# A hybrid streaming layer on one core: the opening with one 96-column product and chunked fill, and the router tile by tile in the output projection

## What is computed

```
h  = RMSNorm(x);  p = h @ W_in            # columns for all branches: qi (1024), ki (64), wi (16), g_lr (16), ...
o_A = sparse attention: scores sum_h wi[t,h] relu(qi[t,h] . ki[s]), top-k keys, softmax over them
o_G = gated linear attention, forget gate from g_lr (rank 16);  o_M = attention into 256 memory tokens
x1 = x + W_out( sum_b sigmoid(gate_b(h)) * (o_b @ W_b) )
y  = x1 + HMoE(RMSNorm(x1))   # top-1 of 4 expert groups, then top-2 of its 8 experts; 32 experts of 3 MB
...
g_logit = hb @ w_group_router + b_group_router;  g_idx = argmax(g_logit)
e_logit = (hb @ w_expert_router + b_expert_router)[group g_idx];  top_p, top_i = top_k(softmax(e_logit), 2)
```

## Time and profile before

| | |
|---|---|
| median of 3 runs | 1762.69 us |
| profiled execution, own time | 1760.87 us |
| its span | 1759.2 us |
| PE busy | 1545.2 us (88%) |
| DVE, ACT, POOL busy | 529.0, 296.1, 109.5 us |
| mean DMA rate | 144 GB/s |

### The profile page before, as it was taken

How to read it: one execution, slowest core, us unless ns; L and a number is a source line. 1 busy time by engine, 2 the same in 40 slices (tenths; PEclk the granted TensorE clock), 3 DMA queues, 4 the chain that set the end, 5 groups by cost and what they waited for, 6 DMA issues and landing times.

```text
span 1759.2 us, 16947 instructions
## 1 busy us (share of the span) xinstructions
PE 1545.2 (88%) x6653; PEld 862.2 (49%) x6653; DVE 529.0 (30%) x1462; ACT 296.1 (17%) x689; POOL 109.5 (6%) x176
## 2 busy tenths in 40 slices
PE   3999999999799999988999999999999728878771
PEld 3554555445455544465555445755544524444440
DVE  3204489205400032442010343244640330101013
ACT  4004310212200011143100112343000201110100
POOL 5000000012000000000000100100000020000002
PEclk9899999999899999999999999999999758998996
DMA  9971121111332325134114130220150347999995
GB/s 259 214 209 37 37 54 31 48 48 49 108 96 72 119 96 191 48 130 158 49 50 141 49 125 11 74 82 27 48 190 5 143 172 278 422 422 421 422 421 201
DMA packets 131256, 253.13 MB, mean 144 GB/s; under 512 B 9840, under 2 KB 87664, under 8 KB 116848
## 3 DMA queue, kind: packets, MB, share of 16 engines
q1 hardware_dynamic: 114352, 183.03, 29.2%
q0 software_dynamic: 16832, 69.12, 12.2%
HBM read 214.21 MB, written 37.91 MB: 143 GB/s over the span
## 4 chain that ended last, share of the span: by engine, by line
PE 76%; DMA 12%; DVE 5%; ACT 3%; issue 2%; POOL 1%; SPq 1%; DVEq 0%; ACTq 0%; POOLq 0%
PE ps L656 21%; DMA arena<-slot_rows 9%; PE ps L678 7%; PE ps L577 6%; PE ps L587 6%; PE ps L606 3%; PE ps L626 3%; PE ps L565 3%; PE ps L1151 2%; PE ps L578 2%; PE ps L588 2%; PE ps L679 2%; PE ps L701 1%; PE ps L1130 1%; PE ps L1054 1%
## 5 line engine op out<-in xcount | busy, mean ns | idle before, releaser
L656 PE MATMUL ps<-bulk 128*128 128x512 f32 x848 | 373.5, 598 | 4.4 <-issue 4.4
L656 PEld LDWEIGHTS ps<-bulk 128*128 128x128 f32 x848 | 160.2, 192 | 196.9 <-issue 196.9
L577 PE MATMUL ps<-bulk 128*128 128x512 f32 x256 | 133.7, 604 | 3.8 <-DMA bulk<-in_w_in 3.8
L678 PE MATMUL ps<-bulk 128*128 128x512 f32 x256 | 135.1, 609 | 0.0
L587 PE MATMUL ps<-arena,bulk 128*128 128x512 f32 x256 | 131.1, 594 | 1.8 <-DVE arena L1660 1.8
L1130 PE MATMUL ps<-bulk,arena 128*64 128x256 f32 x1024 | 116.4, 386 | 9.1 <-DMA bulk<-in_w_exp_gate 8.3
L1130 PEld LDWEIGHTS ps<-bulk,arena 128*64 128x64 f32 x1024 | 81.6, 139 | 49.4 <-issue 22.1
L1151 PE MATMUL ps<-bulk,arena 128*64 128x512 f32 x256 | 71.5, 709 | 11.2 <-ACT arena L1515 11.2
L578 PEld LDWEIGHTS ps<-bulk 128*128 128x128 f32 x256 | 49.4, 193 | 62.6 <-issue 62.6
L1117 PE MATMUL ps<-cst,arena 128*128 128x128 f32 x128 | 20.2, 309 | 66.6 <-DMA arena<-slot_rows 66.6
L679 PEld LDWEIGHTS ps<-bulk 128*128 128x128 f32 x256 | 48.6, 190 | 61.2 <-issue 61.2
(11 more groups left out here) (364 smaller groups left out, 1932.8 us busy)
## 6 DMA issues: line engine op xcount, KB each, us to landing
bulk<-in_w_exp_gate SPq DMA_DIRECT2D x32, 1024.0 KB, 22.5
bulk<-in_w_exp_up SPq DMA_DIRECT2D x32, 1024.0 KB, 24.6
bulk<-in_w_exp_down SPq DMA_DIRECT2D x32, 1024.0 KB, 23.1
bulk<-in_w_in SPq DMA_DIRECT2D x48, 512.0 KB, 5.1
bulk<-in_w_in SPq DMA_DIRECT2D x7, 2048.0 KB, 10.6
slot_rows<-arena POOLq DMA_DIRECT2D x1, 13056.0 KB, 68.1
bulk<-in_w_mem_kv SPq DMA_DIRECT2D x4, 2048.0 KB, 9.5
arena<-slot_rows SPq DMA_DIRECT2D x16, 512.0 KB, 25.9
```

The source lines that it names most:

```text
L577: mm(ps[4 * q + 1][:, 0:TP], tw[2 * q][:, k, :], hT[:, k, 0:TP], start=k == 0, stop=k == KD - 1)
L656: last = mm(ps[4 + n % 2][:, :], lhs[:, k, tok:tok + P], ring[f % 2][:, k, :], start=k == 0, stop=k == KD - 1)
L678: mm(ps[b][:, 0:TP], tw[s][:, k, :], hT[:, k, 0:TP], start=k == 0, stop=k == KD - 1)
```

## The change

**Opening.** On SP the gain `g_x` is issued right behind tile 0, the narrow weights come as three DMAs (`g_lr`, `wi`, `ki`, in this order side by side), and the memory tiles are issued behind the first four indexer blocks. Each token tile has a semaphore of its own, so ACT squares each when it lands. DVE scales tiles 0 and 1, then 2 to 4. PE transposes these five, then makes one product with the 96 narrow columns as the stationary operand (result 96 x tokens), indexer block 0, five small transposes that bring the result back to tokens x 96, block 1, the transposes of the memory tiles, blocks 2 and 3, the transposes of `kid`, and blocks 4 to 7. ACT squares all `ki` at once, and DVE makes one `rstd` and a few wide operations for all five tiles.

**Fill.** The zeros for `slot_rows` go out in 17 DMAs, number c behind narrow block c of the score stage (the last two behind block 15).

**Router.** In the second half of the output projection DVE scales tile t as soon as ACT has squared it; PE puts the transposes of tile t - 1 behind item t and the logits of tile t - 2 into the middle of item t. After the last item the logits of tile 3, the transposes and the logits of tile 4 remain. DVE chooses experts for tiles 0 to 3 and then for tile 4 (`route`), and the rank products of the first four tiles are made between the two. For tile 4 and the totals a sum over four tiles (`hot_sum`) replaces four products by one. `pos_ok` is raised once when the row numbers stand and again after the overflow tables; the softmax weights w0 and w1 are made last. POOL's tables (`iota`) are made after the left half of the projection instead of after all of it.

The diff, cut to what the text speaks of:

```diff
+            for at, col, w in ((0, C_LR, RANK), (RANK, C_WI, HI), (RANK + HI, C_KI, DI)):
+                sp.dma_start(wsm[:, :, at:at + w], w_in[:, :, col:col + w]).then_inc(wsm_in, 16)
...
+            for t in range(NT):
+                x_transposes(t)
+            pe.wait_ge(hT_ok, 2 * NT)
+            pe.wait_ge(wsm_in, 48)
+            for k in range(KD):
+                mm(ps[4][0:NF3, 0:TP], wsm[:, k, :], hT[:, k, 0:TP], start=k == 0, stop=k == KD - 1)
+                last = mm(ps[5][0:NF3, 0:TS], wsm[:, k, :], hT[:, k, TP:T], start=k == 0, stop=k == KD - 1)
+            last.then_inc(kiw_full, 1)
+            indexer_block(0)
...
-            for t in range(NT):
-                if t >= 2:
-                    pe.wait_ge(kid_ok, t - 1)
-                for k in range(KD):
-                    last = mm(ps[2 + t % 2][:, 0:DI + HI], hT[:, k, t * P:(t + 1) * P], wsm[:, k, 0:DI + HI],
-                              start=k == 0, stop=k == KD - 1)
-                last.then_inc(kiw_full, 1)
...
+            for n in index["out"]:
...
+                for k in range(KD):
+                    if c and k == KD // 2 and t >= 2:
+                        if t == 2:
+                            pe.wait_ge(rtw_in, 5 * 16)
+                        router_logits(t - 2)
...
+                if c and t:
+                    h2_transposes(t - 1)
+            router_logits(NT - 2)
+            h2_transposes(NT - 1)
+            router_logits(NT - 1)
...
+            dve.wait_ge(rtw_in, 80)
             for n in index["out"]:
...
+                if c:
+                    ffn_normed(t)
+
+            dve.wait_ge(rt_full, 1)
+            dve.wait_ge(pool_step, 2 + N_TABLES)
+            route(0, NT - 1)
+            dve.wait_ge(rt_full, 2)
+            route(NT - 1, NT)
...
-            g.dma_start(slot_rows.rearrange("(p n) d -> p n d", p=CAP), zrow[0:CAP, :].unsqueeze(1).to_broadcast([CAP, N_SLOT, D]))\
-             .then_inc(fill_ok, 16)
...
+            for c in range(FILLS):
+                j = min(c, 2 * KD - 1)
+                pool.wait_ge(t_full[j % 4], U_QK + j // 4 + 1)
```

More of the change, by code:

```diff
@@ L394, in _ @@
             for t in range(NT):
[L395 to L399, removed]
+                sp.dma_start(xt[:, t, :], x_tile[t]).then_inc(X_IN[t], 16)
+                if t == 0:
+                    sp.dma_start(g_x, a["attn_norm_g"].partition_broadcast(P)).then_inc(gx_in, 16)
+            for at, col, w in ((0, C_LR, RANK), (RANK, C_WI, HI), (RANK + HI, C_KI, DI)):
+                sp.dma_start(wsm[:, :, at:at + w], w_in[:, :, col:col + w]).then_inc(wsm_in, 16)
             def narrow_job(col, u):
@@ L544, in _ @@
[L544 to L567, removed]
+            def indexer_block(j):
+                s, u, b = j % 4, U_QI + j // 4, 2 * (j % 2)
+                pe.wait_ge(tw_in[s], 16 * u)
+                pe.wait_ge(t_free[(s + 2) % 4], u + 1 if s >= 2 else u)
+                for k in range(KD):
+                    mm(ps[b][:, 0:TP], tw[s][:, k, :], hT[:, k, 0:TP], start=k == 0, stop=k == KD - 1)
+                    last = mm(ps[b + 1][:, 0:TS], tw[s][:, k, :], hT[:, k, TP:T], start=k == 0, stop=k == KD - 1)
+                last.then_inc(t_full[s], 1)
@@ new lines, in _ @@
+            for t in range(NT):
+                last = tr(ps[6][:, t * NF3:(t + 1) * NF3], featT[:, t * P:(t + 1) * P], ident[0:NF3, 0:NF3])
+            last.then_inc(kiw_full, 1)
+            indexer_block(1)
+            pe.wait_ge(glr_ok, 1)
+            for m in range(NM):
+                x_transposes(NT + m)
+            indexer_block(2)
+            indexer_block(3)
+            pe.wait_ge(kid_ok, 1)
+            pe.wait_ge(hT_ok, 2 * (NT + NM))
+            for t in range(NT):
+                last = tr(ps[(7, 4)[t // 4]][:, (t % 4) * P:(t % 4 + 1) * P], kid[:, t, :], ident)
@@ L569, in merge_job @@
+            last.then_inc(kidT_full, 1)
+            for j in range(4, KD):
+                indexer_block(j)
+            pe.wait_ge(const_ok, N_CONST)
             def merge_job(u, m, ready, before_branch=None):
@@ L1080, in _, with h2_transposes @@
             pe.wait_ge(merged_ok, 16)
-            project(("out",))
-            n = 0
-            for t in range(NT):
+            def h2_transposes(t):
                 pe.wait_ge(h2_ok, t + 1)
                 for h in range(2):
+                    n = 2 * t + h
                     if n >= 2:
@@ L1100, in _ @@
-            pe.wait_ge(rt_step, 2)
-            for t in range(NT):
-                for s in range(t + 1):
-                    mm(ps[3][:, t * NE:(t + 1) * NE], before if s == t else ones, hot_both[:, s, :], start=s == 0, stop=s == t)
-            for s in range(NT):
-                last = mm(ps[3][:, NT * NE:(NT + 1) * NE], ones, hot_both[:, s, :], start=s == 0, stop=s == NT - 1)
-            last.then_inc(rank_full, 1)
+                    last = mm(lt_bank(t), h2T[:, k, t * P:(t + 1) * P], w_rt[:, k, :], start=k == 0, stop=k == KD - 1)
@@ new lines, in _ @@
+            router_logits(NT - 2)
+            h2_transposes(NT - 1)
+            router_logits(NT - 1)
+            rank = ps[6]
+            pe.wait_ge(rt_step, 1)
+            for t in range(NT - 1):
+                for s in range(t + 1):
+                    mm(rank[:, t * NE:(t + 1) * NE], before if s == t else ones, hot_both[:, s, :], start=s == 0, stop=s == t)
+            pe.wait_ge(rt_step, 2)
+            t = NT - 1
+            mm(rank[:, t * NE:NT * NE], ones, hot_sum, start=True, stop=False)
@@ L1107, in _ @@
+            mm(rank[:, t * NE:NT * NE], before, hot_both[:, t, :], start=False, stop=True)
+            mm(rank[:, NT * NE:(NT + 1) * NE], ones, hot_sum, start=True, stop=False)
+            mm(rank[:, NT * NE:(NT + 1) * NE], ones, hot_both[:, t, :], start=False, stop=True).then_inc(rank_full, 1)
             pe.wait_ge(pos_ok, 1)
@@ L1200, in _, with x_squared @@
                 act.sem_inc(t_free[s], 1)
-            for t in range(NT + NM):
-                act.wait_ge(x_in[min(t, 2)], 16 if t < 2 else 16 * (NT + NM - 2))
+            def x_squared(t):
+                act.wait_ge(X_IN[t], 16 if t < NT else 16 * NM)
                 if t:
@@ L1581, in _ @@
+            dve.wait_ge(kid_ok, 1)
             dve.wait_ge(hT_ok, 2 * (NT + NM))
```

277 lines of the change are left out of this document (168 added, 109 removed).

## The result

| | before | after |
|---|---|---|
| median of the runs, us | 1760.4 (1756.7 to 1765.1) | 1712.2 (1707.7 to 1713.4) |
| ratio, 95% interval | | 0.972 (0.969 to 0.975) |
| profiled execution, span | 1759.2 | 1706.0 |
| scores start | 132.8 | 109.1 |
| projection starts | 1301.2 | 1273.4 |

The change takes 48 us off the median and brings it to 1712.2, where 1711 was forecast. Before was run once more beside after, which is why its median is 1760.4 here and not 1762.7. Two single executions are left out of the medians that follow, because they ran far from the others of their kernel and no trace shows why: 1777.9 us of before with the new router stage, and 4110.7 us of the combined kernel.

A forecast was written before the change was run, and what follows sets the result against it. PE is busy 88% of the span, except in a DMA-full opening and a serial stage before the scatter. 1759.2 - 25.5 (opening) - 26.0 (router) = 1707.7 span, 1711 us median; range 1703 to 1720 (0.74), to 1730 (0.86).

The forecast's parts named there:

- Tile 4 lands at 14.0: Opening: the sample tile lands at 14.0 us, since g_x ahead of it leaves the bytes ahead about the same.
- To the product at 24.1: Opening: square, rstd, three scalings, eight transposes and a copy after tile 4 lands let the 96-column product start at 24.1.
- Eight blocks and the inserted work, 73.6: Opening: eight indexer blocks 69.2 us, plus 4.4 for inserted transposes and a memory-tile wait; scores at 107.4.
- Narrow weights landed in time: Opening: narrow weights land at about 18 to 21 us, needed at 24.1, cover 3 us.
- Fill at 0: 13 MB zero fill beside the narrow blocks at 133 to 313 us: cost 0, at most 5 in the last rounds.
- The middle moves as a block: Between 133 and 1301 us nothing is tied to an absolute time; order unchanged, so it moves as a block.
- Last item 78.9 after the projection's start: Projection: inserted transposes and logits add 8.3 us, so the last item ends at 1380.1 instead of 1371.8.
- Give-back behind the scatter, 1.0: Behind the scatter: expert 3's 3 MB issued 2.1 us later against it; 1.0 of the 27.0 gain given back.
- Late opening: Rival, opening: tile 4 at 19 and product at half clock give 5 + 7.6 us back, 1724; chance 0.12.
- Clock inside the projection: Rival, projection: 36-column products halve the clock for three items, 28 us back, 1739; chance 0.07.
- Weights eat the gain: Rival, experts: weights' bytes limit from 1372 us on, so an earlier scatter buys nothing, 1737; chance 0.03.
- slower by the fill: Rival, narrow blocks: fill gets ahead of their weights; all 68.1 us on PE's path gives 1779; chance 0.02.

The follow-up runs named there:

- the combined kernel: After, with g_x in POOL's queue, narrow weights in two transfers, extra identity transposes in the opening and 216 behind the last rank: 1711.8 us, ratio 0.972.

## Why the prediction was right, point by point

- **Tile 4 lands at 14.0: wrong, 15.9.** The step that failed is "the bytes ahead are about the same". They are, but g_x had moved from a queue beside the tiles into the queue of the tiles; moved back, the tile lands at 13.2 with the same bytes.
- **To the product at 24.1: 27.4.** Of the 3.3 us, 1.9 is the landing; the rest is the transposes of three tiles, 5.7 us at half clock behind one another, where I counted only the last at 1.9.
- **The product, 9.7: 8.7.** Full clock from its first record. The 96 stationary columns cost no more than 128 (8.65 a block).
- **Eight blocks and the inserted work, 73.6: 73.0.** So the scores came at 109.1 instead of 107.4 and the opening gave 23.7 instead of 25.5 us.
- **Narrow weights landed in time: right.** They landed 12.0 and 7.6 us after their issue, and PE never waited. The Trainium skill (DMA: Bandwidth & Descriptors, Specifications) asks for at least 512 B a transfer for line rate. Here SP was held for 11.4 us by three pieces with shorter runs and for 6.4 by two, but no path waited for it; whether the run length or the number of pieces does it, no run separates.
- **Fill at 0: right as a price, incomplete as a reading.** At its new place only POOL waits for it, 8.1 us for the last piece, and its memset is done by 300.4, off the chain. That in one piece at its old place it would have eaten 13 us of the new opening did not stand in the prediction: I took from the earlier trace rows that no engine waited for it in before and did not ask whether that cover, 0.7 us in the end (97.4 to 98.1), would survive the other edit.
- **The middle moves as a block: right within chance.** 1168.5 and 1164.3 us, range of 14 executions 9 us. I gave no term for this scatter beyond the 3 us of the runs.
- **Last item 78.9 after the projection's start: 76.9.** The inserted work is 8.0 instead of 8.3 (76.9 against 68.9 in the kernel with the opening alone). The other 1.7 is the short spell at half clock at the projection's start, in the earlier trace rows and in five of the experiments, which was absent from after's profiled execution: luck.
- **From the last item to the last rank, 18.5: 18.8,** and 5.5 to the scatter against 5.6. The tile chain, the split `route` and the ranks at half clock came as computed: the durations were all in the rows.
- **Give-back behind the scatter, 1.0: 0.7.** Counted from the projection's start, the scatter gained 28.8 us, where 27.0 was forecast, and the first pair's products 28.1; the 1.7 of the absent spell is in both. But the scatter's start was the wrong landmark for the overflow tables: the run with the late scatter moved it by 2.1 us and the pair by 0.2.
- **The rivals.** *Late opening:* the tile 1.9 us late, none of the 7.6 for the product. *Clock inside the projection:* did not happen with 8 products a piece and happens in part with 16. *Weights eat the gain* and *slower by the fill:* not seen, though the second names the mechanism that the whole fill then showed, in the opening and not in the narrow blocks. One sign missed without a cost: PE's first transpose, forecast at about 12, came at 13.7, on a constant of POOL's.

The errors partly cancel. The profiled execution of after came out 1.7 us under my 1707.7 because its middle ran 4 us shorter than in before; the two stages by themselves gave 23.7 + 28.1 - 2.7 = 49.1 us, where 51.5 was forecast. The level has luck of its own: 1711 was built on a median of 1762.7 for before, and on the 1760.4 that stands now the same 51.5 would have said 1708.9. So the gain was forecast 3 us too high, inside the spread of the runs, and the two misses hide each other. The 2.7 above is what the end lags behind expert 4's issue more than in before (291.9 against 289.2 us), both within the spread given above.

## What to carry to other kernels

A transfer that is hidden today is hidden by work of a certain length and place. When another edit shortens that work, price the transfer again, against the new schedule, and look how thin its cover already was. For the first loads of a kernel, count what stands ahead in the same queue, not only the bytes under way. And before trusting a gain of a few us, look at how much an untouched stretch differs from one execution to the next.

## What the runs showed of the hardware that I had not expected

- Narrow products can lower the clock of what comes *after* them, without any idle time: behind 16 products of 36 columns (3.7 to 4.0 us) the next four of 512 columns took 5.1 and 5.4 us instead of 3.7 in two of three items (clock 0.87 and 0.88 of the item); behind 8 of them none of 30 items fell. A group of 32 products of 64 columns took 11.6 us in one execution and 7.4 in another. The Trainium skill's second failure mode (TensorE: Matmul & The Clock Gate) is about short idle times between groups; here PE was busy throughout.
- The length of a wait alone does not tell the clock behind it: transposes ran at full clock after waits of 0.6 and 1.7 us behind the extra ones, and in the combined kernel after 2.2 us behind 64 of them (1.09 us for eight). The ranks ran at half after the same 2.2 us with narrow products before it, the rows' transposes at half after 2.9 us behind 216 transposes without a gap.
- What stands ahead in a tile's own queue counts: 0.5 MB ahead of it there cost it 2.7 us against the same 0.5 MB in another queue, and 1 MB put right behind it cost nothing (15.9 either way).
- A 13 MB transfer of one queue can hold a 0.5 MB transfer of another for 41.9 us. With nothing of the fill beside them such transfers landed in 3.8 to 9.3 us in the opening, and the two issued together with the first pieces of 0.77 MB, at 124.9 and 141.0, in 4.8 and 4.6 us.
- Identical code of about 1165 us differs by up to 9 us from one execution to the next, much of it in spells of lowered clock (52 us at 1.00 or at 0.87).
